# Which engine makes the low parts of the weights: GpSimd only while routing runs, VectorE for all others

## The chip, the cores and the metric

The kernel runs on one core of a Trainium2 chip. The metric is the device time of one execution in microseconds (us), as the median of several runs. One execution is also recorded by the hardware profiler; times inside it are counted from the start of its span.

## What is computed

Two models of two layers each follow one another on a sequence of 256 tokens of width 1024, all in float32. The part of the reference that matters here is the order of stages:

```python
for layer in range(2):                                  # first_block
    if layer == 0: mix = gla_layer_mixer(h, mem, ...)   # gated linear attention + memory attention
    else:          mix = sb_layer_mixer(h, mem, ...)    # stick-breaking attention + memory attention
    h = layer_norm(ALPHA * h + mix, ...)
    h = layer_norm(ALPHA * h + peer(h, w_q, subkeys, u_tab, v_tab), ...)
for l in range(2):                                      # second_block
    x = x + 0.5 * swiglu(rms_norm(x), w_gate, w_up, w_down)
    x = x + concat(neighborhood, difference, grouped-query, dilated attention of rms_norm(x)) @ w_out
    x = x + 0.5 * swiglu(rms_norm(x), ...)
```

`peer` searches for each token and head the 16 best of 128 x 128 experts (top-k over two half keys, then over 256 sums), and adds gelu(x . u) * gate * v over the chosen experts. The kernel computes it densely: all 16384 experts up, a gate matrix that is zero elsewhere, all experts down.

## The kernel before

**Weights.** All weights come as 933 units of 128 x 1024 float32. A unit is two halves of 128 x 512, so there are 1866 halves, numbered j in the order in which TensorE uses them. The product is split for accuracy: a weight half is the sum of a high part WH (float32r) and a low part WL, the activation likewise (XTh, XTl or GH, GL), and TensorE sums three products (high x high, high x low, low x high). For each half four engines work in turn:

- SyncE (`Sync.run`) loads units into RAW, a ring of NRAW = 4 units; a unit's place is loaded again when both its low parts are made.
- ScalarE (`Scalar.split`) copies RAW to WH, a ring of NHALF = 5 halves, when TensorE has spent half j - 5.
- VectorE (`Vector.split`) or GpSimd (`Gpsimd.split`) computes WL = RAW - WH. `low_on_pool(j)` says which of the two; the other engine passes over this j.
- TensorE (`Tensor.half`) waits for WL and uses the half for 12 matmuls of 128x256 (`cols`) or 6 of 128x512 (`depth`; `rows` has 6 or 12 by its width).

**Stages.** `UNITS` lists the units of ten stages, and `BASE` their first half: the keys of the memory and GLA (halves 0 to 73), PEER 0 (74 to 617), SB (618 to 673), PEER 1 (674 to 1217), then feed-forward, MIX, feed-forward, twice (from 1218). A PEER stage has 16 units of queries (32 halves), 128 units up (256 halves) and 128 units down (256). Routing, the top-k search and its decoding on VectorE, runs under the first 64 units up; the gates are made under the last 64 units up and the first 64 units down (GP = 64).

**Order.** Every engine runs the same program skeleton. Each call of `halves(n)` does for each half a `Pace.tick` and then a `split`. A tick advances "foreground" and "background" generators by a budget (`rate`): attention heads, norms, routing, gates. So attention steps and weight halves are interleaved in an order fixed when the program is built, and it is the same on TensorE, ScalarE, VectorE and GpSimd. `split` is called NHALF halves ahead of TensorE's use. Each engine executes in order: an instruction that waits on a semaphore holds up all that is behind it on this engine.

```python
def split(self):                      # Vector; Gpsimd has the test the other way round
    c, e, j = self.c, self.e, self.made
    self.made += 1
    if j < N_HALVES and not low_on_pool(j):
        raw, wh, wl = c.low(j)
        e.wait_ge(*c.hi.at(j))        # ScalarE's copy of this half
        e.tensor_tensor(wl, raw, wh.bitcast(F32), ALU.subtract).then_inc(*c.lo_v.mark(j))
```

**One attention head** (`attention`): TensorE's scores go to one of two banks; VectorE adds the bias, if there is one (L1736), and takes the negated maximum (L1741); ScalarE takes the exponentials of both blocks (L1133); TensorE transposes them (L419) into bank 6, which VectorE (L1749, even heads) or ScalarE (L1142, odd heads) copies out; TensorE multiplies with the values, and VectorE scales the result (L1758, L1764, L1767, L1769). The transposes of the next head need bank 6 free again. In SB (`two_heads`) ScalarE computes the softplus's logarithm (L1298 to L1302), VectorE adds (L1937) and masks (L1943), TensorE sums along the keys into the scores' bank, ScalarE takes the exponential (L1314), and VectorE copies the outputs (L1928). In GLA, L1848 updates the states.

**Who makes the low part before.** Every fourth half (j % 4 == 3) is GpSimd's, except in the gate stretches of the PEER stages and in the second to fifth half of a stage: 329 of 1866.

Of the kernel before, what the change touches and what calls it, by code (L numbers as in the profile page):

```python
# [20 lines left out]
NHALF = 5  # L21
GP = 64
# [5 lines left out]
BASE = [2 * sum(UNITS[0:s]) for s in range(len(UNITS) + 1)]  # L28
GLA, PEER, SBM, FFN, MIX = 0, (1, 3), 2, {(0, 1): 4, (0, 2): 6, (1, 1): 7, (1, 2): 9}, (5, 8)


def low_on_pool(j):

    for layer in range(DEPTH):
        up = BASE[PEER[layer]] + 32 + 2 * GP + NHALF
        if up <= j < up + 4 * (128 - GP):
            return False
    for end in BASE[1:]:
        if end + 1 <= j <= end + 4:
            return False  # L40
    return j % 4 == 3


class Signal:
# [79 lines left out]
class Chip:  # L124
# [77 lines left out]
    def lo(self, j):  # L202
        return (self.lo_p if low_on_pool(j) else self.lo_v).at(j)
# [1362 lines left out]
class Vector:  # L1566
# [6 lines left out]
    def split(self):  # L1573
# [5 lines that stand above are left out]
            e.wait_ge(*c.hi.at(j))  # L1579
            e.tensor_tensor(wl, raw, wh.bitcast(F32), ALU.subtract).then_inc(*c.lo_v.mark(j))  # L1580
# [714 lines left out]
class Gpsimd:  # L2295
# [6 lines left out]
    def split(self):  # L2302

        c, e, j = self.c, self.e, self.made
        self.made += 1
        if j < N_HALVES and low_on_pool(j):
            raw, wh, wl = c.low(j)
            e.wait_ge(*c.hi.at(j))
            e.tensor_tensor(wl, raw, wh.bitcast(F32), ALU.subtract).then_inc(*c.lo_p.mark(j))  # L2309
# [432 lines left out]
```

## Time and profile before

| | |
|---|---|
| median of 3 runs | 3191.75 us (3189.97 to 3192.04) |
| the profiled execution | 3195.57 us, its span 3193.5 us |
| TensorE matmul busy | 3029.3 us, 95% of the span |
| VectorE busy | 2097.6 us, 66% |
| ScalarE busy | 1597.0 us, 50% |
| GpSimd busy | 492.8 us, 15% |
| mean granted TensorE clock | 0.974 |

Matmuls overlap one another and their ends are modelled, so TensorE's busy time says where it had work, not how fast it was. An engine's idle time is put down to the engine that released it last. In the rows PE is TensorE's matmul, PEld its weight load, DVE VectorE, ACT ScalarE, POOL GpSimd.

### The profile page before, as it was taken

The numbers are of one execution on the slowest core, as the hardware profiler recorded it, in microseconds if no ns is written. First come the engines' busy times: TensorE is split into PE (matmuls) and PEld (weight loads), VectorE is DVE, ScalarE is ACT, GpSimd is POOL, SyncE is SP. The second block draws the span as 40 slices with busy tenths as digits, with TensorE's granted clock in tenths as the row PEclk, the third lists the DMA queues.
The fourth block names the chain that finished last, engine by engine and source line by source line (L and its number), as shares of the span: only waits on it lengthen the run. The fifth ranks groups of instructions, "written<-read, shape, count | busy, mean of one in ns | idle before, by whom it ended". The sixth has DMA issues, their size and how long they took to land.

```text
span 3193.5 us, 56060 instructions
## 1 busy us (share of the span) xinstructions
PE 3029.3 (95%) x21820; PEld 2730.7 (86%) x21820; DVE 2097.6 (66%) x4342; ACT 1597.0 (50%) x3039; POOL 492.8 (15%) x371
## 2 busy tenths in 40 slices
PE   8989999999998989999999999799979999998899
PEld 8789999988787879999988888699768989976798
DVE  4559988799655456987879945654665455456544
ACT  5445544444555545554444455455535555553454
POOL 1213210000021112320000022222101213210121
PEclk9999999999999999999999999899989999999999
DMA  6345554444554334554445555455314556542354
GB/s 213 119 146 170 180 166 159 160 161 164 187 192 160 127 122 160 171 173 158 159 159 166 166 198 195 171 187 180 126 59 149 190 181 197 185 141 70 113 188 155
DMA packets 139512, 512.60 MB, mean 161 GB/s; under 512 B 15713, under 2 KB 16242, under 8 KB 137970
## 3 DMA queue, kind: packets, MB, share of 16 engines
q1 hardware_dynamic: 134352, 489.22, 46.6%
q10 hardware_dynamic: 4898, 19.81, 1.7%
q8 instruction: 174, 2.85, 0.4%
q14 instruction: 88, 0.72, 0.1%
HBM read 507.92 MB, written 1.05 MB: 159 GB/s over the span
## 4 chain that ended last, share of the span: by engine, by line
PE 85%; DVE 10%; ACT 3%; issue 1%; DMA 1%; ACTq 0%; DVEq 0%; SPq 0%
PE ps L415 84%; DVE WL L1580 2%; ACT WH L1037 1%; PE ps L419 1%; ACT BIG L1133 1%; DVE BIG L1692 1%; DVE BIG L1741 1%; DMA RAW<-in_w 0%; DVE XTl L1619 0%; DVE BIG L1655 0%; DVE H L1658 0%; DVE BIG L2025 0%; DVE BIG L1986 0%; DVE BIG L2032 0%; DVE BIG L1633 0%
## 5 line engine op out<-in xcount | busy, mean ns | idle before, releaser
L1037 ACT ACTIVATE WH<-RAW 128x512 fp32r<-128x512 f32 x1866 | 1168.5, 630 | 1193.8 <-PE ps L415 1167.1
L1580 DVE TENSOR_TENSOR WL<-RAW,WH 128x512 fp32r<-128x512 f32 x1537 | 1109.7, 725 | 868.6 <-ACT WH L1037 860.7
L415 PE MATMUL ps<-XTh,WH 128*128 128x256 f32 x3928 | 1131.6, 288 | 22.4 <-DVE XTl L1788 8.2
L415 PE MATMUL ps<-XTl,WH 128*128 128x256 f32 x3928 | 1120.6, 285 | 0.0
L415 PE MATMUL ps<-XTh,WL 128*128 128x256 f32 x3928 | 1119.9, 285 | 0.0
L2309 POOL TENSOR_TENSOR WL<-RAW,WH 128x512 fp32r<-128x512 f32 x329 | 441.3, 1341 | 2652.8 <-ACT WH L1037 2652.8
L415 PEld LDWEIGHTS ps<-XTh,WH 128*128 128x128 f32 x3928 | 762.9, 194 | 34.1 <-DVE WL L1580 14.5
L415 PEld LDWEIGHTS ps<-XTl,WH 128*128 128x128 f32 x3928 | 763.5, 194 | 3.1
L415 PEld LDWEIGHTS ps<-XTh,WL 128*128 128x128 f32 x3928 | 762.8, 194 | 0.0
L415 PE MATMUL ps<-WH,GH 128*128 128x512 f32 x1408 | 562.5, 399 | 20.0 <-DVE GL L2100 8.1
L415 PE MATMUL ps<-WL,GH 128*128 128x512 f32 x1408 | 554.0, 393 | 0.0
L415 PE MATMUL ps<-WH,GL 128*128 128x512 f32 x1408 | 553.2, 393 | 0.0
L415 PEld LDWEIGHTS ps<-WH,GH 128*128 128x128 f32 x1408 | 267.3, 190 | 78.1 <-issue 9.8
L415 PEld LDWEIGHTS ps<-WH,GL 128*128 128x128 f32 x1408 | 267.0, 190 | 57.8
L415 PEld LDWEIGHTS ps<-WL,GH 128*128 128x128 f32 x1408 | 267.6, 190 | 50.2
L415 PE MATMUL ps<-BIG 128*128 128x64 f32 (+6 forms) x966 | 154.2, 312 | 23.7 <-DVE BIG L1769 5.8
L415 PEld LDWEIGHTS ps<-BIG 128*128 128x128 f32 (+4 forms) x966 | 124.1, 190 | 48.5 <-issue 22.8
L415 PE MATMUL ps<-WH,XTh 128*128 128x512 f32 (+1 forms) x400 | 158.0, 395 | 4.4 <-DVE XTl L1619 1.3
L415 PE MATMUL ps<-WH,XTl 128*128 128x512 f32 (+1 forms) x400 | 150.1, 375 | 0.0
L415 PE MATMUL ps<-WL,XTh 128*128 128x512 f32 (+1 forms) x400 | 149.9, 375 | 0.0
L419 PE MATMUL ps<-CST,BIG 128*128 128x128 f32 x430 | 78.4, 322 | 61.7 <-DVE BIG L1692 36.6
L419 PEld LDWEIGHTS ps<-CST,BIG 128*128 128x128 f32 x430 | 59.8, 166 | 83.1 <-DVE BIG L1692 41.6
(182 smaller groups left out, 2209.3 us busy)
## 6 DMA issues: line engine op xcount, KB each, us to landing
RAW<-in_w SPq DMA_DIRECT2D x933, 512.0 KB, 3.3
BIG<-in_ln ACTq DMA_DIRECT2D x4, 1024.0 KB, 6.3
GAIN<-in_norms ACTq DMA_DIRECT2D x6, 512.0 KB, 4.1
BIG<-in_sk ACTq DMA_DIRECT2D x2, 1024.0 KB, 5.0
BIG<-in_na_bias ACTq DMA_DIRECT2D x2, 1024.0 KB, 10.2
BIG<-in_qk_gain ACTq DMA_DIRECT2D x2, 960.0 KB, 6.6
BIG<-in_memT ACTq DMA_DIRECT2D x4, 256.0 KB, 7.6
BIG<-in_xT ACTq DMA_DIRECT2D x1, 1024.0 KB, 5.5
```

Source lines behind the costliest of these rows:

```text
L415: return self.e.matmul(out, lhsT, rhs, start=start, stop=stop, skip_group_check=loose)
L419: return self.e.transpose(out, in_, self.c.IDENT[0:n, 0:n])
L1037: e.activation(wh, raw, ACT.Copy).then_inc(*c.hi.mark(j))
L1133: e.activation(t.E[:, i % 3, w], src[:, w], ACT.Exp, bias=s[:, blk:blk + 1], accum_out=s[:, 2 + blk:3 + blk]).then_inc(*c.exps.mark(tag, i ...
L1580: e.tensor_tensor(wl, raw, wh.bitcast(F32), ALU.subtract).then_inc(*c.lo_v.mark(j))
L1692: e.scalar_tensor_tensor(out=c.XN[:, blk, w], in0=c.H[:, blk, w], scalar=s[:, 3:4], in1=c.GAIN[:, w], op0=ALU.mult, op1=ALU.mult).then_inc ...
L1741: e.tensor_reduce(s[:, 0:2], src, AX, ALU.max, negate=True).then_inc(*c.maxed.mark(tag, i))
L2309: e.tensor_tensor(wl, raw, wh.bitcast(F32), ALU.subtract).then_inc(*c.lo_p.mark(j))
```

## The change

`low_on_pool(j)` gets another test. GpSimd makes the low part of the halves with j % 4 == 3 only in the 128 halves whose low parts are made while routing runs, in each of the two PEER stages. VectorE makes the low part of every other half. Nothing else is changed: buffers, loads, ScalarE's copies and the order of all other work stay.

```diff
 def low_on_pool(j):
 
     for layer in range(DEPTH):
-        up = BASE[PEER[layer]] + 32 + 2 * GP + NHALF
-        if up <= j < up + 4 * (128 - GP):
-            return False
-    for end in BASE[1:]:
-        if end + 1 <= j <= end + 4:
-            return False
-    return j % 4 == 3
+        up = BASE[PEER[layer]] + 32 + NHALF
+        if up <= j < up + 2 * GP:
+            return j % 4 == 3
+    return False
```

## Rows read from the trace of the kernel before

**Rows 1.** The page: the chain that ended last, by engine.
```profile
PE 85%; DVE 10%; ACT 3%; issue 1%; DMA 1%; ACTq 0%; DVEq 0%; SPq 0%
```

**Rows 2.** Busy us by stretch (columns as headed): PEER down, SB, feed-forward, MIX.
```profile
core 0: us, PE busy (x) PEld busy (x) DVE busy (x) ACT busy (x) POOL busy (x), PEclk, DMA share, GB/s
...
842.00:1016.00 174.00, 173.71 (x758) 143.07 (x758) 86.12 (x158) 98.77 (x187) 40.22 (x31) 0.99 0.59 195
...
1040.00:1160.00 120.00, 115.41 (x786) 103.19 (x786) 52.25 (x93) 64.63 (x136) 15.73 (x12) 1.00 0.36 115
...
2042.00:2234.00 192.00, 188.21 (x1312) 177.05 (x1313) 97.88 (x151) 101.21 (x184) 53.61 (x45) 0.99 0.61 198
...
2244.00:2410.00 166.00, 144.22 (x741) 114.96 (x741) 100.01 (x210) 72.83 (x184) 18.64 (x14) 0.93 0.30 99
```

**Rows 3.** Groups: count, busy us, mean ns, then idle time before them.
```profile
L1580 DVE TENSOR_TENSOR WL<-RAW,WH 128x512 fp32r<-128x512 f32 x1537 | 1109.7, 725 | 868.6 <-ACT WH L1037 860.7
...
L2309 POOL TENSOR_TENSOR WL<-RAW,WH 128x512 fp32r<-128x512 f32 x329 | 441.3, 1341 | 2652.8 <-ACT WH L1037 2652.8
```

**Rows 4.** Timeline (start, us, what, idle before) of the first MIX, j = 1371.
```profile
2275.28 0.69 DVE L1736 TENSOR_TENSOR BIG<-ps,BIG 128x512 f32<-128x512 f32 x1
...
2276.39 0.61 ACT L1037 ACTIVATE WH<-RAW 128x512 fp32r<-128x512 f32 x1
...
2277.09 1.27 POOL L2309 TENSOR_TENSOR WL<-RAW,WH 128x512 fp32r<-128x512 f32 x1 [10.14 <-ACT WH L1037]
...
2278.54 0.69 DVE L1580 TENSOR_TENSOR WL<-RAW,WH 128x512 fp32r<-128x512 f32 x1 [1.86 <-ACT WH L1037]
...
2279.89 0.42 PEld L419 LDWEIGHTS ps<-CST,BIG 128*128 128x128 f32 x4 [0.44 <-DVE BIG L1749]
```

**Rows 5.** The same stage: timeline around j = 1399, then one stretch's busy time.
```profile
2370.01 0.17 DVE L1610 TENSOR_SCALAR BIG<-BIG 128x8 f32<-128x8 f32 x1
2370.17 1.26 POOL L2309 TENSOR_TENSOR WL<-RAW,WH 128x512 fp32r<-128x512 f32 x1 [13.28 <-ACT WH L1037]
2370.21 1.24 DVE L1612 TENSOR_TENSOR BIG<-BIG 128x8 f32<-128x8 f32 x1
...
2373.03 0.48 PE L419 MATMUL ps<-CST,BIG 128*128 128x128 f32 x1 [3.55 <-DVE BIG L2277]
...
2373.50:2380.00 6.50, 5.77 (x26) 4.60 (x24) 1.46 (x3) 1.19 (x2) 0.00 (x0) 0.63 0.12 45
```

**Rows 6.** Timeline of SB, around j = 647 and j = 651.
```profile
1088.62 0.29 DVE L1928 COPY BIG<-ps 128x128 f32<-128x128 f32 x1 [1.80 <-PE ps L415]
...
1089.58 1.39 POOL L2309 TENSOR_TENSOR WL<-RAW,WH 128x512 fp32r<-128x512 f32 x1 [9.62 <-ACT WH L1037]
...
1089.91 1.13 PE L415 MATMUL ps<-BIG 128*128 128x256 f32 x6
...
1100.35 0.43 DVE L1943 TENSOR_TENSOR BIG<-BIG 128x256 f32<-128x256 f32 x1
...
1100.45 1.46 POOL L2309 TENSOR_TENSOR WL<-RAW,WH 128x512 fp32r<-128x512 f32 x1 [9.48 <-ACT WH L1037]
...
1100.85 0.69 PE L415 MATMUL ps<-BIG 128*128 128x256 f32 x2
```

**Rows 7.** Timeline of GLA, around j = 31.
```profile
60.94 0.69 DVE L1741 TENSOR_REDUCE BIG<-ps 128x2 f32<-128x512 f32 x1 [0.63 <-PE ps L415]
...
61.96 1.27 POOL L2309 TENSOR_TENSOR WL<-RAW,WH 128x512 fp32r<-128x512 f32 x1 [8.68 <-ACT WH L1037]
...
63.95 0.68 DVE L1749 COPY BIG<-ps 128x512 f32<-128x512 f32 x1
...
65.49 0.60 PE L419 MATMUL ps<-CST,BIG 128*128 128x128 f32 x4
```

**Rows 8.** Timeline of GLA, around j = 63.
```profile
138.62 1.30 POOL L2309 TENSOR_TENSOR WL<-RAW,WH 128x512 fp32r<-128x512 f32 x1 [5.57 <-ACT WH L1037]
139.10 1.37 DVE L1580 TENSOR_TENSOR WL<-RAW,WH 128x512 fp32r<-128x512 f32 x1 [2.41 <-ACT WH L1037]
...
141.12 0.50 PE L415 MATMUL ps<-WH,XTh 128*128 128x512 f32 x1 [0.93 <-DVE XTl L1722]
```

## The prediction

> **What bounds the kernel now.** I read the page first, then busy time by stage, then the groups of instructions, then the timeline around each half whose low part changes engine. TensorE carries 85% of the chain that ended last [rows 1]. By stage, a feed-forward stretch has TensorE busy 188.2 of 192 us and the second half of an expert down-projection 173.7 of 174 us, with VectorE at 97.9 and 86.1 us. SB and MIX are looser: TensorE is busy 115.4 of 120 and 144.2 of 166 us [rows 2]. So the places where a change of VectorE's work can show are the waits inside the looser stretches (GLA is one too). There TensorE, ScalarE and VectorE hand attention heads round in a fixed program order, and the weight halves are threaded into the same three queues.
>
> **The change, part by part.** *Count.* By the new test only the halves with j % 4 == 3 in the 128 from BASE + 37 of each PEER stage stay on GpSimd: 32 + 32 = 64. The trace has 329 low parts on GpSimd [rows 3], so 265 move: 18 in GLA, 13 in SB, 14 in each MIX, 32 in each feed-forward, 39 in each PEER stage (8 in the queries, 31 in the second half of the down-projection). GpSimd's low parts under routing, and the gate stretches where it made none, stay as they were.
>
> *Busy time.* One low part takes 725 ns on VectorE as a mean and 1341 ns on GpSimd [rows 3]; with GpSimd idle VectorE takes 0.69 us [rows 4]. VectorE gets 265 x 0.69 = 183 us. A feed-forward stage goes from 97.9 to at most 97.9 + 32 x 0.69 = 120 of 192 us, the down-projection half to 86.1 + 31 x 0.69 = 108 of 174 us [rows 2]. Both stay well under TensorE, and five weight buffers lie between, so I cost the 2 x 39 + 4 x 32 = 206 halves moved there at nothing. What hides them is TensorE's own work, 192 / 132 = 1.45 us per half. With that cover gone 32 x 0.69 = 22 us per feed-forward stage would be the ceiling. The loads are issued by SyncE when both low parts of a unit are made; VectorE's is made sooner than GpSimd's where VectorE is free, and later where it waits, by up to 2.4 us (below), against a ring of 8 halves, or 8 x 1.45 us: nothing.
>
> *What is removed.* Where both engines subtract at once, VectorE's instruction is stretched. In GLA it took 1.37 us beside a GpSimd low part of 1.30 us, and TensorE then waited 0.93 us for the next operand [rows 8]. In one queue the two low parts end at 138.62 + 2 x 0.69 = 140.0 in place of 139.10 + 1.37 = 140.47: 0.46 us back. In MIX a 128x8 instruction of the difference-attention norm took 1.24 us beside a GpSimd low part, where the one before it took 0.17; TensorE waits 3.55 us for the end of this chain [rows 5]. The half concerned (j = 1399) stands behind the chain in VectorE's program, so 1.24 - 0.17 = 1.07 us come back whole, in each MIX stage.
>
> *What is added: a wait in VectorE's queue.* This is the main term. GpSimd had nothing else to do, so its wait for ScalarE's copy cost nobody. On VectorE the low part stands in program order, and what is behind it waits until ScalarE has made the copy, which ScalarE does only after the exponentials of earlier heads. I placed each moved low part in VectorE's program (behind the pace's tick for its half) and compared the end of its copy with the start of the VectorE instruction behind it. Mostly VectorE was idle there anyway. Four have a price that can reach TensorE.
> 1. MIX, j = 1371, and its twin in the second MIX. The copy runs from 2276.39 for 0.61 us, and GpSimd starts at 2277.09. The low part belongs ahead of the bias add of head 2 that ran at 2275.28, so this add moves to 2277.09 + 0.69 = 2277.78, or 2.5 us. Behind it, link by link, come the maximum, the exponentials, the next copy, the low part at 2278.54 and the probability copy L1749, for which TensorE's next transposes (2279.89) already wait [rows 4]. Some 0.2 us of slack sit at the exponentials. I take +2.3 us each.
> 2. SB, j = 647. VectorE would end at 1089.58 + 0.69 = 1090.27; behind it are an output copy that ran at 1088.62, the softplus sum and the mask, and TensorE's sum along the keys at 1089.91 starts right behind the mask [rows 6]. I take +1.6 us.
> 3. SB, j = 651: 1100.45 + 0.69 = 1101.1, then a second output copy (0.2) and the same links as before from copy to TensorE (1089.91 - 1088.62 = 1.3), hence 1102.6. Before, the mask ended at 1100.78 and TensorE started at 1100.85 [rows 6]. I take +1.7 us.
> 4. GLA, j = 31: the maximum of head 2 moves from 60.94 to 61.96 + 0.69 = 62.65, or 1.7 us. The probability copy, 63.95 + 0.68 = 64.63, moves with it, and TensorE needs it at 65.49, 0.86 us later [rows 7]. I take +0.9 us.
>
> The same reading gives delays of 1 to 2.4 us at three more places of each MIX and at four of SB, but there the result is not wanted yet, or the stretch that goes away pays for it; and there are delays and gains under 0.7 us. I take 0 for all of them; their bounds are -1 and +4 us together.
>
> *Sum.* Two MIX stages: 2 x (2.3 - 1.07) = +2.5. SB: 1.6 + 1.7 = +3.3. GLA: 0.9 - 0.46 = +0.4. Together +6.2 us. The profiled execution took 3195.57 us (span 3193.5, 2.1 around it), so it would take 3201.8. The median of the runs shown, 3191.75, lies 3.8 us under it and becomes **3198.0 us**.
>
> *The clock.* Behind the 3.55 us wait in MIX the granted clock is 0.63 over 6.5 us, that is, for much of them 1.2 instead of 2.4 GHz; without this dip up to (1 - 0.63) x 6.5 = 2.4 us come back per MIX [rows 5]. The wait gets shorter and may lose its dip; new waits of 1.6 to 2.3 us may bring dips of up to the same price. I take zero net, and keep -4.8 and, for the five new waits, +12 us as bounds.
>
> *A rule against this forecast.* The stretched 128x8 instruction ended at 2371.45, the GpSimd one beside it at 2371.43 [rows 5]. The Trainium skill ("SBUF — State Buffer", section "Who interferes with whom") says that a VectorE instruction with two SBUF inputs and a GpSimd instruction that reads SBUF exclude each other, the later one blocked for the whole of the other. On this row the trace agrees. By this rule alone each overlap that goes is a gain, and the sum would hold only the gains (the first rival).
>
> **The rivals.**
> *The relief decides (faster).* The place is the norm chain of each MIX and the operand in GLA, the price -(2 x 1.07 + 0.46) = -2.6 us, and with both clock dips gone -2.6 - 4.8 = -7.4: 3184 to 3189 us. It decides if the waits at the four places stay hidden and a dip goes too. For it speaks that the 3.55 us wait is real and its chain VectorE's alone; against it, that in MIX and SB TensorE starts within 0.1 us of VectorE's end.
> *Slack absorbs both.* TensorE has 21.8 us of other idle time in a MIX stage [rows 2], and a delay ahead of a wait for something else vanishes in it. That gives -3 to +3 us, about 3192. Against it, most of those waits are for results of the delayed engines.
> *The blocks cost more.* New waits bring clock dips, or places that I set to zero reach TensorE: +10 to +16 us, 3202 to 3208.
> *VectorE becomes the bound in the dense stages.* 22 us per feed-forward stage is the ceiling, a few us each likelier: 3210 and more. The 120 of 192 us speak against it.
> That the change doesn't do what it says is left out: the test is arithmetic on j.
>
> **How the numbers follow.** About 0.2%, 6.4 us here, is what a measurement of this kernel can tell from no change. The forecast (+3 to +10 us, 3195 to 3202) has a chance of 0.55; its centre lies by that bound, so it splits into 0.28 slower and 0.27 same. The costlier blocks have 0.15 (slower), slack 0.20 (same), the relief 0.07 (0.04 faster, 0.03 same), VectorE as bound 0.03 (slower). So faster 0.04, same 0.50, slower 0.46. The range of 3189 to 3205 leaves out the lost dips below and the far half of the costlier blocks above, under 2 in 10.
>
> **What would show it.** VectorE has 1802 low parts and GpSimd 64, and VectorE's mean falls. In MIX the bias add of head 2 follows a low part, with a TensorE wait of about 2.3 us for the probability copy, and the 3.55 us wait is about 2.5. In SB two TensorE waits of about 1.6 us for the mask appear. Feed-forward and PEER stages keep their length. I am wrong if these waits are absent or recovered within their stage, if dips come and go by more than the waits, or if TensorE waits for low parts in the dense stages.

## The result, and the profile after

The changed kernel takes 3203.32 us (median of 6 runs, 3199.13 to 3207.5), the kernel before in the same rounds 3191.89 us. The ratio is 1.0037, 95% interval 1.0024 to 1.005: **slower by about 11.8 us** (7.7 to 16.0, the ratio times 3192). The profiled execution took 3201.17 us, its span 3199.1. Line numbers of the changed kernel are 3 lower than before.

The page's chain by engine and its groups of low parts, against [rows 1, 3]:

```profile
PE 82%; DVE 11%; ACT 4%; issue 2%; DMA 1%; ACTq 0%; DVEq 0%; SPq 0%
...
L1577 DVE TENSOR_TENSOR WL<-RAW,WH 128x512 fp32r<-128x512 f32 x1802 | 1264.9, 706 | 774.1 <-ACT WH L1034 760.9
...
L2306 POOL TENSOR_TENSOR WL<-RAW,WH 128x512 fp32r<-128x512 f32 x64 | 93.2, 1458 | 1160.5 <-ACT WH L1034 1160.5
```

1802 + 64 low parts, as counted, and VectorE's mean fell from 725 to 706 ns. Busy time by stretch, each from the stage's first matmul to that of the next: GLA, the second half of a down-projection, SB, feed-forward, and the two MIX stages (against [rows 2]):

```profile
core 0: us, PE busy (x) PEld busy (x) DVE busy (x) ACT busy (x) POOL busy (x), PEclk, DMA share, GB/s
38.50:160.90 122.40, 116.41 (x640) 92.60 (x639) 68.94 (x123) 61.30 (x124) 3.81 (x3) 0.99 0.39 132
844.20:1016.70 172.50, 172.21 (x759) 141.96 (x759) 107.73 (x188) 98.70 (x187) 0.00 (x0) 1.00 0.58 196
1041.70:1163.90 122.20, 115.77 (x785) 103.31 (x786) 55.30 (x105) 63.83 (x134) 0.00 (x0) 1.00 0.31 109
2046.80:2239.50 192.70, 187.63 (x1312) 175.90 (x1313) 112.99 (x183) 101.18 (x183) 11.77 (x13) 0.99 0.57 197
2250.10:2412.90 162.80, 144.49 (x741) 117.24 (x742) 105.00 (x223) 72.98 (x183) 0.00 (x0) 0.93 0.30 101
2824.00:2993.20 169.20, 149.56 (x740) 120.24 (x741) 105.22 (x223) 72.70 (x183) 0.00 (x0) 0.90 0.29 97
```

VectorE is far from full in the dense stretches (107.7 of 172.5, 113.0 of 192.7 us), and TensorE fills both as before. The two MIX stages run the same program with the same new wait, yet differ by 6.4 us. TensorE is busy 5.1 us longer in the second, at a granted clock of 0.90 instead of 0.93. (The clock is given as a share of the full 2.4 GHz; its lower level, 1.2 GHz, is 0.50.)

The first MIX at j = 1371 (timeline; compare [rows 4]):

```profile
2281.50 0.62 ACT L1034 ACTIVATE WH<-RAW 128x512 fp32r<-128x512 f32 x1
...
2282.15 0.69 DVE L1577 TENSOR_TENSOR WL<-RAW,WH 128x512 fp32r<-128x512 f32 x1 [1.68 <-ACT WH L1034]
...
2282.76 0.68 DVE L1733 TENSOR_TENSOR BIG<-ps,BIG 128x512 f32<-128x512 f32 x1
...
2285.84 0.69 DVE L1577 TENSOR_TENSOR WL<-RAW,WH 128x512 fp32r<-128x512 f32 x1 [1.68 <-ACT WH L1034]
2286.45 0.68 DVE L1746 COPY BIG<-ps 128x512 f32<-128x512 f32 x1
...
2287.19 0.44 PEld L416 LDWEIGHTS ps<-CST,BIG 128*128 128x128 f32 x4 [2.64 <-DVE BIG L1746]
```

VectorE stands idle for 1.68 us until the copy of this half comes, then the low part, then the bias add that was ready long before. TensorE waits 2.64 us where it waited 0.44: +2.20. Instruction by instruction, the second MIX adds 2.21. The other waits, SB at j = 647 and 651 and GLA at j = 31 (timelines; compare [rows 6, 7]):

```profile
1090.29 0.69 DVE L1577 TENSOR_TENSOR WL<-RAW,WH 128x512 fp32r<-128x512 f32 x1 [2.71 <-ACT WH L1034]
...
1090.90 0.28 DVE L1925 COPY BIG<-ps 128x128 f32<-128x128 f32 x1
...
1092.16 0.51 PEld L412 LDWEIGHTS ps<-BIG 128*128 128x128 f32 x3 [1.53 <-DVE BIG L1940]
...
1102.67 0.69 DVE L1577 TENSOR_TENSOR WL<-RAW,WH 128x512 fp32r<-128x512 f32 x1 [4.39 <-ACT WH L1034]
...
1104.74 0.51 PEld L412 LDWEIGHTS ps<-BIG 128*128 128x128 f32 x3 [1.67 <-DVE BIG L1940]
...
62.31 0.69 DVE L1577 TENSOR_TENSOR WL<-RAW,WH 128x512 fp32r<-128x512 f32 x1 [1.61 <-ACT WH L1034]
...
66.56 0.66 PE L416 MATMUL ps<-CST,BIG 128*128 128x128 f32 x4 [0.51 <-DVE BIG L1746]
```

Aligned with the trace of before, TensorE falls back there by 1.49, 1.63 and 0.67 us.

### The profile page after: what moved, and what is told of

The parts are those of the page before. It is cut to its first block, busy times and chain, and to the rows that moved or that the text cites. A ratio compares the mean times of both kernels' runs of the same rounds, so it can differ in the third digit from the quotient of the medians.

```text
span 3199.1 us, 56058 instructions
## 1 busy us (share of the span) xinstructions
PE 3032.1 (95%) x21820; PEld 2733.6 (85%) x21820; DVE 2241.2 (70%) x4607; ACT 1597.6 (50%) x3039; POOL 144.4 (5%) x106
## 4 chain that ended last, share of the span: by engine, by line
PE 82%; DVE 11%; ACT 4%; issue 2%; DMA 1%; ACTq 0%; DVEq 0%; SPq 0%
PE ps L412 81%; DVE WL L1577 3%; ACT WH L1034 1%; PE ps L416 1%; DMA RAW<-in_w 1%; ACT BIG L1130 1%; DVE BIG L1738 1%; DVE BIG L1689 1%; DVE XTl L1616 0%; DVE BIG L2029 0%; DVE BIG L1652 0%; DVE H L1655 0%; DVE BIG L2022 0%; DVE BIG L2033 0%; DVE BIG L1983 0%
## 5 line engine op out<-in xcount | busy, mean ns | idle before, releaser
L1577 DVE TENSOR_TENSOR WL<-RAW,WH 128x512 fp32r<-128x512 f32 x1802 | 1264.9, 706 | 774.1 <-ACT WH L1034 760.9
L2306 POOL TENSOR_TENSOR WL<-RAW,WH 128x512 fp32r<-128x512 f32 x64 | 93.2, 1458 | 1160.5 <-ACT WH L1034 1160.5
## 6 DMA issues: line engine op xcount, KB each, us to landing
BIG<-in_na_bias ACTq DMA_DIRECT2D x2, 1024.0 KB, 10.4
```

## The experiments

Three theories. **Queue theory**, the prediction's: the cost is the order in VectorE's queue at five halves (31, 647, 651, 1371, 1695), 0.7 + 1.5 + 1.6 + 2 x 2.2 = 8.2 us of waits, less some relief elsewhere. **Amount** (rival A): each moved half costs the same, 11.4 / 265 = 0.043 us. **Clock and chance** (rival B): TensorE's granted clock, and which engine happens to start first in routing, decide. Each kernel was run 5 to 12 times, the two repeats once, and its ratio is against runs of the kernel before made beside it. Each is the kernel before with another test, except that of experiment 3; the helpers are

```diff
+# old_on_pool(j): the test of the kernel before, unchanged
+def routing(j):
+    ups = [BASE[PEER[layer]] + 32 + NHALF for layer in range(DEPTH)]
+    return j % 4 == 3 and any(up <= j < up + 2 * GP for up in ups)
+def loose(j):
+    return any(BASE[k] <= j < BASE[k + 1] for k in (GLA, SBM) + MIX)
```

**1. Where do the 11 us come from: four parts of the change.**

```diff
+    return old_on_pool(j) if loose(j) else routing(j)   # e1: only the dense stages move
+    return old_on_pool(j) and not loose(j)              # e2: only GLA, SB, MIX move
+    return old_on_pool(j) and j not in FIVE             # e3: only 31, 647, 651, 1371, 1695 move
+    return routing(j) or j in FIVE                      # e4: the change, those five kept
```

> Only the 206 halves of the PEER and feed-forward stages move to VectorE; in GLA, SB and MIX GpSimd keeps its low parts. Queue theory (the cost is VectorE waiting for ScalarE's copy in front of attention work, at five halves): 0 us against before, within 2. Rival A (each moved half costs the same, 11.4 / 265 = 0.043 us): +8.9 us. Rival B (any shift of phase changes which of GpSimd and VectorE is stretched under routing, and the clock dips): +2 to +5 us, with most of it in the routing stretches.

> Only the 59 halves of GLA, SB and the two MIX stages move. Queue theory: +6 to +11 us, nearly all of the change's cost. Rival A: 59 x 0.043 = +2.5 us. Rival B: +2 to +5 us, part of it under routing.

> Only five halves move: j = 31, 647, 651, 1371, 1695. Queue theory: the waits read in the changed kernel's trace, 0.7 + 1.5 + 1.6 + 2.2 + 2.2 = +8.2 us, without the gains elsewhere. Rival A: +0.2 us. Rival B: +2 to +5 us.

> The change, but these five halves stay on GpSimd. Queue theory: 11.4 - 8.2 = +3 us against before, or about -2 us if the rest of the 11.4 also hangs on them. Rival A: +11.2 us. Rival B: +2 to +5 us with new stretches under routing.

| kernel | halves moved | ratio (interval) | us |
|---|---|---|---|
| e1, dense only | 206 | 0.9999 (0.999 to 1.0008) | -0.3 |
| e2, loose only | 59 | 1.0032 (1.002 to 1.0044) | +10.2 |
| e3, five only | 5 | 1.0051 (1.0037 to 1.0065) | +16.3 |
| e4, five kept | 260 | 1.0006 (0.9997 to 1.0015) | +1.9 |

(us is the ratio less 1, times 3193, here and below.) Amount falls: 206 moved halves cost nothing, five cost 16. Of rival B's +2 to +5 us for any shift, e1's interval leaves room up to +2.6. The cost sits at the five, and it is twice their waits when they move alone.

**2. The five in two pairs, and the relief alone.** The halves 1371 and 1695 are each the 22nd of the 60 halves of its MIX stage, one in each of the two stages.

```diff
+    return old_on_pool(j) and j not in (647, 651)                          # f1
+    return old_on_pool(j) and j not in (1371, 1695)                        # f2
+    return old_on_pool(j) and j not in (19, 63, 1383, 1399, 1707, 1723)    # f3
```

> Only the two halves of SB, j=647 and j=651, move to VectorE. Queue theory: two waits of TensorE of 1.5 and 1.6 us (as long as in the whole change), so +3.1 us. If a new wait also costs TensorE's clock wherever it falls, more than that: in the run of the five halves the time rose by twice the waits, which here would be +6. If only the number of moved halves counts (0.043 us each), +0.1.

> Only the last halves of layer 0 in the two MIX stages, j=1371 and 1695, move. Queue theory: two waits of 2.2 us, +4.4 us, and with the run of the other pair and GLA's 0.7 this adds up to 8.2. The five halves together gave +16.3; if the surplus is the clock granted in the MIX stages (28 and 37 us at 1.2 GHz there against 14 to 17), then it belongs to this pair alone: +9 to +12 us here, with the longer stretches at 1.2 GHz in both MIX stages. If only the number of moved halves counts, +0.1.

> Only the halves move whose low part TensorE waits for after GpSimd's addition of the bias (j=19, 63, 1383, 1399, 1707, 1723). Queue theory: the waits end earlier by 2 x 1.07 in MIX at j=1399 and 1723, 0.46 at j=63 and 2 x 0.15 at j=1383 and 1707: -2.9 us; more, down to -6, if a stretch at 1.2 GHz in MIX goes with them. The rival that slack behind these waits absorbs the gain: 0. If VectorE, the busier engine, hands the earlier end back at the next reduction: 0 as well, and its wait would show at L2277.

SB's pair alone: 1.0014 (1.0005 to 1.0022), +4.5 us, with 3.1 inside the interval (and the 6 of a clock loss too; the traces decide below). MIX's pair alone: 1.003 (1.0019 to 1.0041), +9.6 us, twice its waits of 4.4. The relief alone: 0.9997 (0.9989 to 1.0006), -1.0 us, which neither shows -2.9 nor excludes it. The windows of SB with its pair moved (first fence), and of the two MIX stages with theirs (second), with ten microseconds up to the wait at j = 1371 and the four behind it:

```profile
1041.90:1164.40 122.50, 115.81 (x786) 103.30 (x787) 51.40 (x95) 63.84 (x134) 12.86 (x10) 1.00 0.33 110
```

```profile
2249.10:2417.50 168.40, 145.68 (x740) 116.99 (x741) 100.39 (x210) 72.62 (x183) 17.34 (x13) 0.93 0.30 97
2829.40:2997.80 168.40, 145.69 (x741) 117.01 (x742) 100.42 (x210) 72.69 (x183) 17.35 (x13) 0.93 0.30 97
...
2276.00:2286.00 10.00, 8.20 (x38) 5.43 (x35) 5.62 (x9) 4.32 (x14) 0.00 (x0) 1.00 0.23 73
2286.30:2290.30 4.00, 3.93 (x17) 3.54 (x18) 2.19 (x6) 2.57 (x7) 0.00 (x0) 0.58 0.00 0
```

SB is longer by its waits and no more (119.3 to 122.5 us), at clock 1.00, and so it is in the other four profiles with these two waits (122.3 to 122.5 us). In MIX the 2.2 us wait is followed by a clock of 0.58 over 4 us, which is mostly the lower level of 1.2 GHz. The full clock of 1.00 stood there before.

This fall comes with the wait. Take in each MIX stage the 4.5 us from 37.0 us behind its first matmul. In the profiles of the six kernels and repeats in which j = 1371 and 1695 hold VectorE up (after, after again, e2, e3, f2, g1) the granted clock is 0.50 to 0.83 there, in all twelve MIX stages. In the eight others it is 1.00 in all sixteen, and experiment 3's kernel, with the same instructions in another order, is one of them. So a wait's follow-up cost depends on the stage: none in SB, where TensorE is busy 115 of 119 us, some in MIX, where it is busy 144 of 165. Which property of the stages makes the difference no run separates; the waits are not equally long either.

How much it costs needs more than one trace. f2's two MIX stages take 168.4 us each, 2.9 to 3.0 more than the 165.5 and 165.4 of before. But e3, which moves the same pair, also without relief in MIX, has 170.3 and 172.5 us (clock 0.92 and 0.89). The ten MIX stages of the profiles in which no half of MIX moved take 162.7 to 166.2 us, 164.7 as a mean; the four of f2 and e3 take 169.9. That is +5.2 us a stage for a wait of 2.2, and 10.4 for the pair, where its time says +9.6. The timed runs agree: their mean granted clock is 0.9726 for f2 and 0.9763 for the kernel before beside it, for f1 0.9758. Not all that f2's own trace has is the pair's: its second routing stage takes 200.8 us instead of 196.1, and it runs ahead of both moved halves.

What the relief does is seen in the second MIX: TensorE's waits for VectorE, in total us, times and the longest, in the second profile of the kernel before (experiment 5) and with the relief halves moved (same lines, 16 higher):

```profile
PE ps L419 <- DVE BIG L2277: 3.5, 1, 3.5
...
PE ps L419 <- DVE BIG L1749: 2.1, 1, 2.1
...
PE ps L415 <- DVE BIG L1769: 1.8, 2, 1.3
...
PE ps L415 <- DVE BIG L2210: 1.5, 2, 0.7
```

```profile
PE ps L435 <- DVE BIG L2293: 2.5, 1, 2.5
PE ps L435 <- DVE BIG L1765: 2.1, 1, 2.1
PE ps L431 <- DVE BIG L1785: 1.8, 2, 1.3
PE ps L431 <- DVE BIG L2226: 1.8, 2, 1.0
```

The norm chain's wait is 1.0 us shorter, as predicted, and one of the three others 0.3 longer: 8.9 us before, 8.2 after, and the stage 163.3 and 162.7. The first profile of the kernel before has 3.5, 0.6, 2.9 and 0.7 in these lines, and 165.4 us: two executions of one kernel differ more than the relief is worth. In GLA it is cleanest, at clock 1.00 in both: at j = 63 TensorE waits 0.34 us where it waited 0.93 [rows 8], and the stage takes 119.4 us instead of 120.0.

```profile
140.98 0.50 PE L431 MATMUL ps<-WH,XTh 128*128 128x512 f32 x1 [0.34 <-DVE XTl L1738]
```

The four MIX stages with the relief and without the pair (f3, and e4, which moves MIX's other halves too) take 163.2 us as a mean, 1.5 less than the ten in which nothing moved. So the relief is there, about as large as predicted, and too small to show in the time alone.

**3. The order alone.** The whole change, with as many instructions on each engine, but VectorE makes the low part of a half of the five one half later, behind the work that it had held up:

```diff
+        if j in LATER:                # (31, 647, 651, 1371, 1695)
+            return
+        if j - 1 in LATER:
+            self.low_part(j - 1)
         if j < N_HALVES and not low_on_pool(j):
+            self.low_part(j)
```

> The whole change, but VectorE makes the low parts of the five halves (31, 647, 651, 1371, 1695) one half later, ahead of the next half's low part, so that they stand behind the maximum or the copy that was delayed. As many instructions on each engine as in the change, only their order differs. Queue theory: SB's two waits go (-3.1 us against the change), MIX's shrink from 2.2 to about 0.7 each (-3.0), GLA's 0.7 goes: about -7 us, -9 with the clock that comes back, so 3194 to 3197 us and +2 to +5 against the kernel before. If what counts is how many low parts VectorE makes: as the change, +11.

Measured: 1.0005 (0.9997 to 1.0014), +1.6 us, where the change has +11.8. The same place in the first MIX, whose wait is back to 0.42 us:

```profile
2282.73 0.61 ACT L1034 ACTIVATE WH<-RAW 128x512 fp32r<-128x512 f32 x1
2283.38 0.69 DVE L1588 TENSOR_TENSOR WL<-RAW,WH 128x512 fp32r<-128x512 f32 x1 [0.81 <-ACT WH L1034]
2283.99 0.68 DVE L1757 COPY BIG<-ps 128x512 f32<-128x512 f32 x1
...
2284.72 0.20 PEld L416 LDWEIGHTS ps<-CST,BIG 128*128 128x128 f32 x2 [0.42 <-DVE BIG L1757]
```

The clock behind this place, in the first and the second MIX, 37.5 to 41.5 us into the stage:

```profile
2286.90:2290.90 4.00, 3.36 (x21) 2.50 (x20) 3.08 (x8) 2.32 (x6) 0.00 (x0) 1.00 0.35 110
2861.90:2865.90 4.00, 3.36 (x21) 2.54 (x21) 2.24 (x6) 3.13 (x8) 0.00 (x0) 1.00 0.12 17
```

SB is 119.2 us again, the MIX stages are 163.6 and 165.7. GLA is not shorter: it takes 124.9 us although its wait is gone, at clock 0.96. The clock is 0.52 there from 41.5 to 48.5 us, ahead of j = 31 and where this kernel's order is still that of the change (whose clock was 1.00 there), so this is chance. This run speaks for the queue theory most plainly: five instructions moved by one place return 10 of the 12 us.

**4. Does relief shrink the MIX pair's cost? And what of the halves that stayed?**

```diff
+    return old_on_pool(j) and not any(BASE[k] <= j < BASE[k + 1] for k in MIX)   # g1
+    return old_on_pool(j) and not routing(j)                                     # g2
```

> All GpSimd halves of the two MIX stages move, and no other. Queue theory: waits of 2 x 2.2 us at j=1371 and 1695, less 2 x 1.07 at j=1399 and 1723 and 2 x 0.15 at 1383 and 1707: +2.0 us. If the relief is real only where nothing gives it back, so that medians add up (the pair alone +9.6, the relief alone -0.8): +8.8. If the clock granted in MIX follows how much TensorE waits there in all, so that relief cuts the pair's surplus: +2 to +5, and about 163 to 167 us for each MIX stage, where the pair alone had 168.4.

> The kernel before, but the 64 halves of the routing stages, the only ones that the change left on GpSimd, move as well, and no other. VectorE is busy 91% of these stages (177 of 194 us); 16 more low parts in each of four stages are 11 us more where it has 17 us left, while GpSimd's calls beside it, which stretch its own, go. Queue theory: about a half of these low parts stands in front of a step of routing that TensorE waits for, 0.7 us each: +10 to +25. If the stretch of VectorE's calls by GpSimd's is worth more than the calls (the wait of 2.4 us at the end of routing goes, which comes in some executions): 0 to -5.

g1: 1.0015 (1.0006 to 1.0024), +4.8 us: below the +8.8 of added medians, within what the third view expected, though the stages in its profile (167.6 and 168.9 us at clock 0.90; its slowest run) were longer than that view said. The interval touches the +2.0 of bare waits too.

g2: **0.9981 (0.9971 to 0.9991), -6.1 us**, the one kernel that beats both (median 3188.58 us), where +10 to +25 was forecast. The first routing stage, low parts of VectorE, in the kernel before (first) and with the routing halves moved too:

```profile
L1580 DVE TENSOR_TENSOR WL<-RAW,WH 128x512 fp32r<-128x512 f32 x91 | 72.2, 799 | 10.5 <-ACT WH L1037 9.9
```

```profile
L1593 DVE TENSOR_TENSOR WL<-RAW,WH 128x512 fp32r<-128x512 f32 x121 | 87.9, 734 | 2.7 <-ACT WH L1050 2.6
```

The change left 64 there, 32 in each of two stages, not 16 in each of four. Thirty more low parts cost VectorE 15.7 us, 0.52 each, because the others fell from 799 to 734 ns as a mean; and VectorE had 10.5 us of waits for copies, of which 7.8 filled up. The stage is 192.6 us, not 193.2, with VectorE busy 184.8 of it, and the second one 195.5, not 196.1. In the first, TensorE's waits for low parts fall from 5.2 us to 3.3, and that for the last reduction (L2045, here L2058) grows from 0.5 to 2.4, so it is not this wait that went.

These 1.2 us are a part of the 6.1 only. The thirteen profiles with GpSimd's low parts under routing have 391.7 us for the two stages as a mean, this one 388.0, because a wait of 2.3 us, to which experiment 5 returns, lengthens some of theirs. Where the rest comes from is not shown; the mean granted clock of the timed runs is 0.978 here and 0.975 for the kernel before.

**5. The same kernels again.**

> The kernel before, unchanged, for a second profile. If the wait at the end of routing (2.4 us, on L2045) and the length of the MIX stages are a matter of the single execution, they differ from the first profile: MIX stages of 162.5 to 166 us and the wait there or not. If they belong to the kernel's order, they are as in the first: 165.5, 165.4, and no wait.

> The changed kernel, unchanged, for a second profile. The waits at the five halves are a matter of order and come again at the same length (GLA 0.7, SB 1.5 and 1.6, MIX 2.2 twice), within 0.1 us. What is a matter of the single execution differs: the wait of 2.4 us at the end of routing, and the MIX stages, 162.8 and 169.2 us in the first profile.

Before again: 3192.78 us, span 3190.6. After again: 3204.04 us, span 3201.9. The five waits came again (0.68, 1.49, 1.62, 2.20, 2.18 us). GLA, SB and the MIX stages, before again and after again:

```profile
38.00:158.70 120.70, 115.96 (x639) 92.70 (x638) 61.67 (x111) 61.20 (x124) 22.05 (x16) 0.99 0.41 134
1039.70:1159.10 119.40, 115.54 (x786) 103.37 (x787) 52.22 (x93) 63.88 (x134) 15.74 (x12) 1.00 0.34 114
2243.90:2409.80 165.90, 144.64 (x740) 115.46 (x741) 99.66 (x209) 72.47 (x184) 18.64 (x14) 0.94 0.30 99
2821.40:2984.70 163.30, 141.65 (x741) 113.44 (x742) 99.86 (x209) 72.60 (x183) 18.63 (x14) 0.96 0.31 100
```

```profile
36.70:160.60 123.90, 117.98 (x639) 93.78 (x638) 68.86 (x123) 61.34 (x124) 3.81 (x3) 0.97 0.39 131
1045.40:1167.70 122.30, 115.85 (x785) 103.39 (x786) 55.38 (x105) 63.82 (x134) 0.00 (x0) 1.00 0.33 109
2252.00:2415.40 163.40, 145.09 (x741) 117.51 (x742) 104.99 (x223) 72.88 (x183) 0.00 (x0) 0.92 0.31 100
2826.80:2996.00 169.20, 149.58 (x740) 120.24 (x741) 105.31 (x223) 72.72 (x183) 0.00 (x0) 0.90 0.29 97
```

A MIX stage of the kernel before may take 163.3 or 165.9 us in one execution, at clock 0.96 or 0.94: the clock and the stage's length go together. The changed kernel's two MIX stages came out nearly as in its first profile (163.4 and 169.2 us, 162.8 and 169.2 there), so their difference was not chance alone. The wait at the end of routing (2.3 us, for the reduction at L2045) is in neither routing stage of the first profile of before and in the second stage of its other profile; of after it is in the second stage of the first profile and the first stage of the other. It comes and goes in both kernels; whether the change makes it more frequent, two profiles each can't show.

## Why the prediction was right, point by point

The range (3189 to 3205) held the time, and slower was nearly as likely as same; the central 3198.0 was 5 us low. The median of 3203.3 lies just above the forecast's own 3195 to 3202 and in the range of a rival, the costlier blocks (3202 to 3208), which had 0.15. What it named, new waits that bring clock dips, is what came on top of the forecast's waits. There is luck in one agreement: 3201.8 was forecast for the profiled execution and it took 3201.17. The 3.8 us taken off from there to the median did not carry over, for the changed kernel's profiled execution lay 2.2 us under its median. The profiled executions differ by 5.6 us, the medians by 11.4.

- **The waits** came where they were placed and about as long: MIX 2.2 twice (2.3 predicted), SB 1.5 and 1.6 (1.6, 1.7), GLA 0.7 (0.9). In two profiles of each kernel SB takes 119.3 and 119.4 us before, 122.2 and 122.3 after: +2.9 for the 3.3 predicted. Shown by the order alone (experiment 3).
- **The dense stages at nothing**: right, -0.3 us for 206 halves (interval -3.2 to +2.6). VectorE as the bound is out.
- **The relief** at j = 1399 and 1723: the wait for the norm chain is 1.0 us shorter in the second MIX, as predicted (2.5 in place of 3.5 us, in f3 and in the changed kernel), and other waits give 0.3 of it back. At j = 63 TensorE waits 0.6 us less, and the stage is 0.6 us shorter (0.46 predicted). Alone the relief bought no time that the runs can tell (-3.5 to +1.9).
- **Places set to zero**: one in GLA, j = 55, was not free: six state updates behind the low part end 0.7 us later for TensorE, in both profiles. What the others did is not separated from the clock.
- **The clock at zero net** is the step that was mis-sized. GLA, SB and MIX together take 0.4 + 3.3 + 2.5 = 6.2 us more by the sum. The two profiles give, as means, GLA 120.35 to 123.15 (+2.8), SB +2.9 and both MIX stages together 330.05 to 332.3 (+2.25), 8.0 in all, and 8.5 for the span (3192.05 to 3200.5). In GLA the moved halves add 1.1 us where the clock stays at 1.00 (e2's profile); the rest came at clock 0.99 and 0.97. In MIX two profiles each are too few: by the stages of nine profiles (experiment 2) the pair costs 10.4 us, of which 4.4 are waits and the rest goes with the lower clock, and the relief gives 3.0 back; with both moved (after, after again, e2, g1) a MIX stage takes 166.3 us as a mean, +3.2 us for the two. Timed in parts, SB cost 4.5, MIX 4.8, and the loose stages together 10.2. Without relief beside it (e3) the five took 16.3 for 8.2, with it about 9.9 (the change less e4). These two differ by 6 us with intervals of 4 to 5 each way, so that relief and clock work on each other is likely, not shown. The runs' own mean granted clock fell from 0.976 to 0.9725. One sign of being wrong that was named, dips that change the time by more than the waits, came for MIX's pair: 5.2 us over its 4.4 of waits.
- **The rule against it**: wrong for this kernel's sum. The relief it promises is real (VectorE's mean fell), but only when the low parts under routing moved too did the kernel get faster (g2), and a part of that gain only is traced to the routing stages.

Open: how the 11.8 us of the change divide. Its two profiles show 8.5, and the same stage in the same order differs between executions by up to 3.1 us (MIX) and 4.7 us (routing). A kernel with the same waits at a fixed clock was not tried.

## What to carry to other kernels

Before work is moved onto an engine that executes in order, look at what it will wait for and what then stands behind it: five of 265 moved instructions carried most of the cost, and 10 of 12 us came back when these five went one place further down the queue. Look at each moved instruction's wait, not at the engine's busy share. And price a helper engine by what it does to the other's instructions: GpSimd's 32 low parts per routing stage saved VectorE only 0.52 us each, and the kernel was 6 us faster without them.

## What the runs showed of the hardware

Which engine starts first decides who pays. The end of routing in the kernel before (first profile; GpSimd's line first) and in the changed kernel:

```profile
1411.58 2.91 POOL L2309 TENSOR_TENSOR WL<-RAW,WH 128x512 fp32r<-128x512 f32 x1 [5.74 <-ACT WH L1037]
...
1411.52 1.21 DVE L2036 TENSOR_TENSOR BIG<-BIG 128x1024 f32<-128x1024 f32 x1
1412.66 0.68 DVE L1580 TENSOR_TENSOR WL<-RAW,WH 128x512 fp32r<-128x512 f32 x1
```

```profile
1413.51 1.45 POOL L2306 TENSOR_TENSOR WL<-RAW,WH 128x512 fp32r<-128x512 f32 x1 [4.85 <-ACT WH L1034]
...
1413.73 1.77 DVE L1577 TENSOR_TENSOR WL<-RAW,WH 128x512 fp32r<-128x512 f32 x1
```

VectorE ahead by 0.06 us: its instructions keep 1.21 and 0.68 us, GpSimd's takes 2.91, where one alone takes 1.28. GpSimd ahead by 0.22: VectorE's takes 1.77 in place of 0.68, another further on 1.61, and TensorE waits 2.3 us for the end of the chain. By the Trainium skill ("SBUF — State Buffer", section "Who interferes with whom") the one that issues later is blocked for the whole of the other; the trace agrees roughly, 1.77 in place of the 1.9 us that the 1.2 left of GpSimd's 1.45 and its own 0.68 make. The wait of 2.3 us came in 12 of the 26 routing stages of all profiles with GpSimd's low parts in them.

A wait of 2.2 us was followed by a stretch at 1.2 GHz in MIX, in twelve stages of twelve, while two of 1.5 and 1.7 us in SB were not, in five profiles. Two MIX stages with the same instructions and the same wait took 162.8 and 169.2 us in one execution. So short waits can have a price that the wait's own length doesn't show, and that no single profile gives.
